# In the last mixer of a hybrid block and in all that follows it, work is done on the 256 grid tokens alone, and the mixer has 12 attention units instead of 18

## The reference

```python
def second_block(...):
    h = concatenate([meta_tokens, x])              # 16 + 256 = 272 tokens, 1024 features
    for l in range(2):
        h = h + 0.5 * swiglu(rms_norm_2(h, ffn1_norm[l]), ffn1_w_in[l], ffn1_w_out[l])
        h = h + hybrid_mixer(rms_norm_2(h, mix_norm[l]), w_in[l], ...)
        h = h + 0.5 * swiglu(rms_norm_2(h, ffn2_norm[l]), ffn2_w_in[l], ffn2_w_out[l])
    return rms_norm_2(h, final_norm)[:, META:]

def hybrid_mixer(n, ...):
    qa, ka, va, qb, kb, vb, qc, kc, vc, gates = split(n @ w_in)
    oa = window_sink_attention(...)      # 8 heads of 64, window of 128 and meta keys, with a sink
    ob = neighbourhood_attention(...)    # 8 heads, neighbourhood on the grid, and meta keys
    oc = dense_block_attention(...)      # 8 heads, 2 key heads, all tokens
    up = branches @ w_branch             # 3 branches, 512 -> 1024 features each
    return sum(sigmoid(gates) * up) @ w_out
```

## Time and profile before

| | us |
|---|---|
| median of 3 runs | 2606.12 |
| lowest and highest | 2604.53, 2606.26 |
| the profiled execution | 2606.43 |
| its span | 2604.3 |
| TensorE busy in the span | 2435.4 |

### The profile page before, as it was taken

One profiled execution on the slowest core, in us unless ns is written; L12 is line 12 of the kernel. 1 busy time (PEld: TensorE's weight loads), 2 busy tenths in 40 slices (PEclk: granted clock), 3 DMA queues, 4 the chain that ended last, 5 costly groups with the idle time before them and its releaser, 6 DMA issues. The chain is left out here.

```text
span 2604.3 us, 47231 instructions
## 1 busy us (share of the span) xinstructions
PE 2435.4 (94%) x19417; PEld 2340.7 (90%) x19417; DVE 1711.7 (66%) x2555; ACT 1122.8 (43%) x1610; POOL 103.7 (4%) x139
## 2 busy tenths in 40 slices
PE   7878899997988999989999999999999999999998
PEld 6878799997768999979988889999999888898998
DVE  5674577764565777667765656677777655656775
ACT  4734433324555333253335554533433356545332
POOL 1031000000000000000031000000000220000000
PEclk8889899998898999989999999999999999999999
DMA  8410355547513555345563233555455452334552
GB/s 218 130 66 29 105 178 193 182 140 133 166 33 101 184 188 193 130 132 176 182 158 118 82 114 130 171 185 170 145 171 187 138 159 87 98 130 155 185 172 70
DMA packets 295126, 370.29 MB, mean 142 GB/s; under 512 B 15337, under 2 KB 263778, under 8 KB 294946
## 3 DMA queue, kind: packets, MB, share of 16 engines
q1 hardware_dynamic: 289728, 354.91, 41.7%
q0 software_dynamic: 4880, 13.13, 2.9%
q10 hardware_dynamic: 370, 0.11, 0.0%
HBM read 360.26 MB, written 7.86 MB: 141 GB/s over the span
## 5 line engine op out<-in xcount | busy, mean ns | idle before, releaser
L302 PE MATMUL psum_banks<-source_high,weights_high 128*128 128x272 f32 (+1 forms) x3680 | 1083.8, 295 | 64.3 <-DVE weights_low L1469 23.8
L304 PE MATMUL psum_banks<-source_high,weights_low 128*128 128x272 f32 (+1 forms) x3680 | 1067.2, 290 | 0.0
L303 PE MATMUL psum_banks<-source_low,weights_high 128*128 128x272 f32 (+1 forms) x3680 | 1067.1, 290 | 0.0
L302 PEld LDWEIGHTS psum_banks<-source_high,weights_high 128*128 128x128 f32 x3680 | 713.0, 194 | 75.8 <-issue 30.7
L303 PEld LDWEIGHTS psum_banks<-source_low,weights_high 128*128 128x128 f32 x3680 | 713.3, 194 | 0.8
L304 PEld LDWEIGHTS psum_banks<-source_high,weights_low 128*128 128x128 f32 x3680 | 712.0, 193 | 0.0
L1469 DVE TENSOR_TENSOR weights_low<-weight_ring,weights_high 128x2048 fp32r<-128x2048 f32 x104 | 239.4, 2303 | 180.1 <-ACT weights_high L1462 179.5
L302 PE MATMUL psum_banks<-hidden_high,weights_high 128*128 128x272 f32 (+1 forms) x1216 | 352.4, 290 | 4.3 <-DVE normed L1076 2.6
L304 PE MATMUL psum_banks<-hidden_high,weights_low 128*128 128x272 f32 (+1 forms) x1216 | 350.4, 288 | 0.0
L303 PE MATMUL psum_banks<-hidden_low,weights_high 128*128 128x272 f32 (+1 forms) x1216 | 349.3, 287 | 0.0
L672 DVE TENSOR_TENSOR weights_low<-weight_ring,weights_high 128x2048 fp32r<-128x2048 f32 x131 | 292.8, 2287 | 74.1 <-ACT weights_high L666 74.0
(11 more groups left out here) (424 smaller groups left out, 2815.9 us busy)
## 6 DMA issues: line engine op xcount, KB each, us to landing
weight_ring<-ffn_w_in SPq DMA_DIRECT2D x88, 1024.0 KB, 6.6
weight_ring<-w_in SPq DMA_DIRECT2D x48, 1024.0 KB, 5.3
weight_ring<-ffn_w_out SPq DMA_DIRECT2D x44, 1024.0 KB, 5.0
weight_ring<-moe_w_gate SPq DMA_DIRECT2D x32, 1024.0 KB, 5.8
weight_ring<-moe_w_up SPq DMA_DIRECT2D x32, 1024.0 KB, 7.2
weight_ring<-moe_w_down SPq DMA_DIRECT2D x32, 1024.0 KB, 4.9
weight_ring<-gdn_w_in SPq DMA_DIRECT2D x16, 1024.0 KB, 5.8
weight_ring<-w_branch SPq DMA_DIRECT2D x12, 1024.0 KB, 5.0
```

Source lines behind the costliest of these rows:

```text
L302: pe.matmul(out, w_hi, x_hi, start=start, stop=False)
L303: pe.matmul(out, w_hi, x_lo, start=False, stop=False)
L304: return pe.matmul(out, w_lo, x_hi, start=False, stop=stop)
```

## The change

Two token ranges get names, `ALL` (0 to 272) and `GRID` (16 to 272), and the helpers of the dense products, of the norm between phases and of the last SwiGLU get an argument `toks`. In the second layer's mixer (`final`), the tiles from 29 on and all that is made of them use `GRID`; a branch has 4 units (`per`), so the loop has 12, by a table `GRID_FILL` of its own. The last `ffn_phase` and `final_phase` use `GRID` as well. Tiles 0 to 28 stay at 272 columns, since keys and values of the meta tokens are needed. Buffers keep their sizes: a row of `GRID` starts 16 elements into the row of 272. Number, order and size of the weight panels and their transfers stay.

```diff
+ALL, GRID = slice(0, L), slice(META, L)
...
-                mm = split_matmul(pe, ps[:, bank, 0:L], hi[:, k, cols], lo[:, k, cols],
-                                  relay.hi[:, k, :], relay.lo[:, k, :], k == 0, k == KT - 1)
+                mm = split_matmul(pe, ps[:, bank, toks], hi[:, k, cols], lo[:, k, cols],
+                                  relay.hi[:, k, toks], relay.lo[:, k, toks], k == 0, k == KT - 1)
...
-                    mm = split_matmul(pe, ps[:, 4 + j % 4, 0:L], hi[:, m, cols], lo[:, m, cols],
-                                      hid_hi[:, par % 2, m, :], hid_lo[:, par % 2, m, :], m == 0, m == 1)
+                    mm = split_matmul(pe, ps[:, 4 + j % 4, toks], hi[:, m, cols], lo[:, m, cols],
+                                      hid_hi[:, par % 2, m, toks], hid_lo[:, par % 2, m, toks], m == 0, m == 1)
...
+        toks = self.toks(t)
...
-            mm = split_matmul(pe, pr.ps[:, bank, 0:self.n_tok], w_hi[:, k, :], w_lo[:, k, :], hi[:, k, :], lo[:, k, :], k == 0, k == kt - 1)
+            mm = split_matmul(pe, pr.ps[:, bank, toks], w_hi[:, k, :], w_lo[:, k, :], hi[:, k, toks], lo[:, k, toks], k == 0, k == kt - 1)
...
-N_UNITS = len(FILL)
+GRID_FILL = [([19], [20], [21]), ([22], [23], [24]), ([25, 26], [27], []), ([28], [29], [30]), ([31], [32], [33]), ([34], [35], [36]),
+             ([37, 38], [39], [40]), ([41, 42], [43], [44]), ([45, 46], [47], [48]), ([49, 50], [51], [52]), ([53, 54], [55], [56]),
+             ([57, 58], [59], [60])]
...
-    def __init__(self, n):
-        self.branch, at = n // 6, n % 6
+    def __init__(self, n, per):
+        self.branch, at = n // per, n % per
...
+    final = layer == DEPTH - 1
+    per, toks, unit_fill = (4, GRID, GRID_FILL) if final else (6, ALL, FILL)
+    n_units = 3 * per
+    rest = max(t for part in unit_fill[-1] for t in part) + 1
...
+        lin = TileStream(pr, relay.w_hi, relay.w_lo, 12 + 3 * 6 + 4, L, {VT_CA: 2, VT_B: 3}, mixes, hands_on=True,
+                         toks=lambda t: toks if t >= GATE_TILES[0] else ALL)
...
-                gemm(63)
-                weigh(N_UNITS - 1)
+                for t in range(rest, 64):
+                    gemm(t)
+                weigh(n_units - 1)
...
-                    if u == 7:
+                    if u == per + 1:
                         dve.wait_ge(pr.bias_in.sem, pr.bias_in.at(16 * 32))
...
-                ffn_phase(pr, relay, "ffn2", l, 0, gain("ffn1", 1), l < DEPTH - 1)
+                ffn_phase(pr, relay, "ffn2", l, 0, gain("ffn1", 1), l < DEPTH - 1,
+                          GRID if l == DEPTH - 1 else ALL)
```

More of the change, by code:

```diff
@@ L545, in low, with square @@
-    def low(self, dve, k, gain):
+    def square(self, act, k, squares, toks=ALL):
+        act.activation(squares[:, k, toks], self.pr.h[:, k, toks], ACT.Square).then_inc(self.squared.sem, 1)
+    def low(self, dve, k, gain, toks=ALL):
         dve.wait_ge(self.made_hi.sem, self.made_hi.at(k + 1))
-        dve.scalar_tensor_tensor(self.lo[:, k, :], self.pr.h[:, k, :], self.pr.params[:, gain + k:gain + k + 1],
-                                 self.hi[:, k, :].bitcast(F32), ALU.mult, ALU.subtract).then_inc(self.made_lo.sem, 1)
@@ L576, in taken, with ffn_phase @@
         self.ready.passed(1)
-def ffn_phase(pr, relay, kind, l, first_slot, gain, split):
+def ffn_phase(pr, relay, kind, l, first_slot, gain, split, toks=ALL):
     nc, ps, h, n_chunks = pr.nc, pr.ps, pr.h, FF_CHUNKS
@@ L743, in _ @@
                 down(pe, last, last)
-                relay.sums(pe, squares)
+                relay.sums(pe, squares, toks)
             @block.scalar
@@ L773, in _ @@
                     if split:
-                        relay.high(act, k, gain)
-                    relay.square(act, k, squares)
+                        relay.high(act, k, gain, toks)
+                    relay.square(act, k, squares, toks)
             @block.vector
@@ L803, in _ @@
                     step(c, c)
-                add_down(dve, last, last, (lambda k: relay.low(dve, k, gain)) if split else None)
+                add_down(dve, last, last, (lambda k: relay.low(dve, k, gain, toks)) if split else None)
     for s, per in ((hm, 2), (sd, 2), (hd, 2), (gm, 2), (um, 2), (dm, 8), (ad, 8), (hi_n, 3), (lo_n, 3), (steps, 4)):
@@ L2537, in hybrid_mixer @@
     rows_b = 2 * ROWS - 1
-    units = [HybridUnit(n) for n in range(N_UNITS)]
-    total = lambda count: [sum(count(x) for x in units[:n]) for n in range(N_UNITS + 1)]
+    final = layer == DEPTH - 1
+    per, toks, unit_fill = (4, GRID, GRID_FILL) if final else (6, ALL, FILL)
+    n_units = 3 * per
+    rest = max(t for part in unit_fill[-1] for t in part) + 1
+    units = [HybridUnit(n, per) for n in range(n_units)]
+    total = lambda count: [sum(count(x) for x in units[:n]) for n in range(n_units + 1)]
     parts, act_ev, dve_ev = total(lambda x: x.parts), total(lambda x: x.act_evicts), total(lambda x: x.dve_evicts)
@@ L2795, in _ @@
                 scores_of(1)
-                for u in range(N_UNITS):
-                    if u + 2 < N_UNITS:
+                for u in range(n_units):
+                    if u + 2 < n_units:
                         scores_of(u + 2)
-                    fill(FILL[u][0])
+                    fill(unit_fill[u][0])
                     if u:
@@ L3108, in _ @@
                 normalise(0)
-                for u in range(N_UNITS):
-                    if u + 2 < N_UNITS:
+                for u in range(n_units):
+                    if u + 2 < n_units:
                         max_of(u + 2)
-                    for t in FILL[u][0]:
+                    for t in unit_fill[u][0]:
                         take(t)
@@ L3122, in _ @@
                             do(dve.tensor_tensor(bias[:, t], bias[:, t], near, ALU.add))
-                    for t in FILL[u][1] + FILL[u][2]:
+                    for t in unit_fill[u][1] + unit_fill[u][2]:
                         take(t)
-                take(63)
-                out_low(N_UNITS - 1)
+                for t in range(rest, 64):
+                    take(t)
+                out_low(n_units - 1)
                 for t in range(64, BRANCH_TILES[2]):
```

118 lines of the change are left out of this document (60 added, 58 removed).

## The result

| | us |
|---|---|
| before, median of 4 runs | 2606.19 (2604.53 to 2611.29) |
| after, median of 4 runs | 2573.76 (2569.59 to 2578.19) |
| ratio, 95% interval | 0.987 (0.9855 to 0.9885) |
| the profiled execution of after, its span | 2574.89, 2572.9 |
| forecast | 2577.0 (2571 to 2585) |

The account below looks back on a forecast made before the run. TensorE's instructions were taken to bound nearly all of the changed part. 16.1 - 0.3 + 10.6 + 0.8 + 1.0 + 1.5 + 0.3 - 1.0 + 0.2 = 29.2 us off 2606.4 gave 2577.2, median 2577.0, range 2571 to 2585.

Parts of the forecast that it names:

- meta units, restarts, other waits: Last mixer's loop: six meta units go, 10.6 us; six fewer switches, 0.8; a wait for ScalarE's turned probabilities nearly goes, 0.3.
- columns, last SwiGLU: Last SwiGLU: 1584 products with 256 columns instead of 272, each 6.1 ns shorter, save 9.7 us.
- columns, gates and branch tiles of the loop: Tiles 29 to 62 of the last mixer's loop: 624 products, each 6.1 ns shorter, save 3.8 us.
- wait at tile 37: Last mixer's loop: TensorE's 2.0 us wait for the panel's low part on VectorE shrinks by 1.0 us.
- clock fall behind it: Behind tile 37's wait: the granted clock's fall goes with half the wait; 1.5 us, bounds -1.7 and 1.5.
- set aside for late starts: Last mixer's loop: 1.0 us reserved for late starts with VectorE and ScalarE fuller in each unit; bounds 0 and 6.
- row sums and the end: End of the kernel: the norm's square, root and reciprocal have 256 columns; saves 0.2 us.
- Nothing is lost and the waits go: Rival, last mixer's loop: no late start and no wait at tile 37, so 2574 us; chance 0.12.
- The offset of 16 elements: Rival, all 2640 products: reads starting 64 bytes in are slow; 2630 us at 20 ns more each; chance 0.03.
- bound by VectorE: Rival, last mixer's loop: late starts reach 6 us and the clock falls once more, so 2585 us; chance 0.15.
- the columns are cheap: Rival, all dense products: weight loads set the pace, columns save about 5.5 us, so 2587; chance 0.07 together with transfers.
- transfers set the pace: Rival, last SwiGLU: panel transfers set its pace, its 9.7 us go, so 2587; chance 0.07 together with cheap columns.

Follow-up runs that it names:

- The SwiGLU alone: Kernel before with only the last SwiGLU and final phase on the 256 grid tokens, last mixer unchanged (18 units, 272 columns); 2594.8 us, ratio 0.9943.

## Why the prediction was right

Of the changed part, 34.1 us against 29.2, by the prediction's own steps. The measured column is read from start times: the SwiGLU's 1584 products take 190.3 us for 202.2; the loop's terms make its 19.5 us, with "meta units, restarts, other waits" what the rest leaves. The longer fall: at the start of the last SwiGLU after is at the lower level of the clock for 5.1 us, before for 3.4.

| step | forecast | measured |
|---|---|---|
| columns, last SwiGLU | 9.7 | 12.7 |
| a longer clock fall at its start than before | 0 | -0.9 |
| columns, gates and branch tiles of the loop | 3.8 | 4.7 |
| columns, the other 432 products | 2.3 | about 2.2 |
| meta units, restarts, other waits | 11.7 | 12.5 |
| wait at tile 37 | 1.0 | 0.8 |
| clock fall behind it | 1.5 | 1.5 |
| set aside for late starts | -1.0 | 0 |
| row sums and the end | 0.2 | 0.6 |
| sum | 29.2 | 34.1 |

**Columns: the mechanism right, the size too small.** This is the term that was mis-sized: 6.1 ns a product, where the SwiGLU shows 8.0 and the loop 7.6. The step that failed is "The first block's experts, the same three products with 256 columns": they have the same columns, but their rows lie otherwise in their buffers. 272 columns were measured in rows 1088 bytes apart (126.0) and 256 in the experts' 1024 bytes apart (119.9); in rows 1088 bytes apart 256 columns take 118.0 to 118.6 in the SwiGLU and the experts. 2640 x 1.9 would be 5.0 us; 3.8 show. In the mixer the products take 118.3 to 118.7, and behind the loop the waits for VectorE grew by 0.6 us in brackets (2.2 to 2.8) where 0.3 was taken off for them. The two prices from the Trainium skill ("TensorE: Matmul & The Clock Gate", section "Back-to-back issue gap") gave estimates of 5.5 and 17.6 us for all columns. Measured are 19.6, so the case falls outside both, nearer to the steeper slope; and the constants of that section fit neither 118.0 nor 126.0.

**The rivals.** The measured median lies on the 2574 of "Nothing is lost and the waits go", but not by its mechanism: nothing was lost to late starts, as it says, yet 1.35 us of the wait at tile 37 stayed, and the rest of the difference is columns. That the two agree to 0.2 us is luck. The offset of 16 elements costs nothing; with it the products are 0.3 to 0.6 ns faster. The loop isn't bound by VectorE: 80 us behind tile 37 have no wait, and the takes (VectorE's reading of a finished tile, which frees its bank) came in time with three tiles in every unit. That the columns are cheap, and that transfers set the pace, is refuted by the SwiGLU's 190.4 us (192.5 forecast).

**The loop.** 169 us were forecast for 186.0; by the same ends, shifted by 2.7, they are 166.5 (2140.7 to 2307.2). The difference of 2.5 is columns (1.0), the reserve that wasn't needed (1.0), and 0.8 in restarts and small waits less 0.2 at tile 37. The 0.8 can be split: the kernel with 18 units and grid columns puts the units, restarts and waits together at 13.7 us. Of these the meta units are 10.6 (the estimate from the earlier trace rows; no run took them out by themselves), the wait at tile 37 is 1.1 (2.48 to 1.35), and the wait of 0.89 us that became 0.25 is 0.6, where 0.3 was counted. 1.4 stay for six restarts, where 0.8 was counted.

**The clock: right in this execution, and partly by luck.** The fall behind tile 37 went, and the forecast tied that to the shorter wait. The kernels with before's mixer and a full wait of 2.13 us there show that it can stay away with the full wait too. The SwiGLU alone, behind the wait at 2145 and behind tile 37:

```profile
2147.50:2152.50 5.00, 5.00 (x29) 4.97 (x28) 3.95 (x8) 3.96 (x14) 0.00 (x0) 0.66 0.56 190
2229.00:2234.00 5.00, 3.26 (x25) 2.77 (x25) 3.93 (x7) 4.32 (x11) 0.00 (x0) 1.00 0.29 81
```

The fall stands behind the first wait and not behind the second, in the same instructions in which before had it the other way round (1.00 from 2148 to 2153 there, 0.66 behind tile 37). The kernel with 18 units and grid columns has it behind the later wait in the first layer and behind neither in the last. In no profiled execution is there one behind both. Behind waits of 2.1 us or more at tile 37, in both layers, 4 of 14 have a fall; behind the 1.35 us 0 of 6. So these runs don't show whether the shorter wait can have one; the 1.50 us at the loop's second unit has one in 6 of 12. What the change removed is a chance of 1.5 us, not 1.5 us. After's second execution has a fall at 2149 and is 1.5 us longer in the loop for it.

## What to carry to other kernels

A price taken from another stage of the same kernel is a good one only if the operands lie the same way there, not only if the shapes agree: equal products cost 116.7 to 120.0 ns in different buffers of this kernel. And padding that pays in one stage is to be measured again in the next, since here it cost in one. Work of the bounding engine that reaches no output (the meta units) is worth its own time on that engine, 10.6 of the 13.7 us here, and how the rest is dealt out was worth nothing in this loop. When one wait stays after a change, look for what stands ahead of the releasing operation on its engine and move that; here one unit earlier gave 3.0 us, by the starts, in two places.

## What the runs showed of the hardware

Products with 256 columns of fp32r, three in turn with a weight load each, start 120.0 ns apart in the experts when their moving rows lie 1024 bytes apart, with almost no scatter. They start 118.6 ns apart at 1088 bytes (118.3 from 64 bytes on) with scatter from 115 to 122, and 118.9 at 1152 bytes. Over the experts' 4608 products 1.4 and 1.7 ns are 6.5 and 8 us; the medians lie 7.7 and 10.0 apart. In the sparse layer's projections the same products start 116.7 ns apart at 1024 bytes and 118.8 at 1088. Why is not shown: with the distance the runs also changed where the high and low rows and all later buffers lie, and no run holds one of these still. Whether anything of it shows at 272 columns (126.0 at 1088 bytes) wasn't tried at another distance.

Behind equal waits of 1.5 and 2.1 us the granted clock falls to the lower level for 3.4 us in one execution and not in the next. One such fall costs 1.5 us, and this is part of why the executions of one kernel lie up to 9.8 us apart.
